# Turning activations in a transformer block: transposes inside the quadrants, and the quadrants exchanged by sixteen SBUF transfers

## The reference

```
h = rms_norm(x, g);  proj = h @ w_in;  gates = sigmoid(h @ w_gate)
merged = g_ret * (ret @ w_ret) + g_att * (att @ w_att)
x = x + merged @ w_out
u = square(relu(rms_norm(x, g2) @ w_up))       # 2048 -> 8192
x = x + u @ w_down                             # 8192 -> 2048
return rms_norm(x, g_final)
```

## Time and profile before

| what | value |
|---|---|
| median of 3 runs | 1591.18 us (1590.75 to 1592.46) |
| span of the profiled execution | 1587.2 us; no own time of it is given beside the span, the runs' median is 4.0 us above it |
| TensorE busy | 1567.3 us, 99% |
| VectorE busy | 1101.6 us, 69% |
| ScalarE busy | 739.1 us, 47% |
| DMA | 301.40 MB, mean 190 GB/s |

### The profile page before, as it was taken

The page is one execution under the profiler, slowest core; times in us unless marked ns, Lnnn a source line. Parts: engine busy times, 40 slices in busy tenths (PEclk is TensorE's granted clock), DMA queues, the critical chain, the costliest instruction groups (busy, mean ns, idle before and its releaser), DMA issues.

```text
span 1587.2 us, 18857 instructions
## 1 busy us (share of the span) xinstructions
PE 1567.3 (99%) x6992; PEld 1292.0 (81%) x6992; DVE 1101.6 (69%) x1398; ACT 739.1 (47%) x983; POOL 10.8 (1%) x17
## 2 busy tenths in 40 slices
PE   9999999999999999999999999999999999999998
PEld 7877778888888888888878888888888888888886
DVE  7877777544447776666699888458864687548855
ACT  6455555444444454444444444444444445444443
POOL 0000000000000000000000000000000000000000
PEclk9999999999999999999999999999999999999999
DMA  9645454565655555556555665565656565555562
GB/s 365 197 134 160 157 159 151 179 201 185 232 179 185 185 190 173 187 192 211 198 201 193 206 209 186 190 199 183 197 189 201 175 203 188 200 194 183 189 203 89
DMA packets 149606, 301.40 MB, mean 190 GB/s; under 512 B 4784, under 2 KB 4912, under 8 KB 149040
## 3 DMA queue, kind: packets, MB, share of 16 engines
q1 hardware_dynamic: 149120, 299.65, 57.0%
q10 hardware_dynamic: 432, 1.02, 0.2%
HBM read 298.55 MB, written 2.10 MB: 189 GB/s over the span
## 4 chain that ended last, share of the span: by engine, by line
PE 88%; DVE 8%; issue 2%; ACT 1%; DMA 0%; SPq 0%; POOLq 0%; DVEq 0%; POOL 0%; ACTq 0%
PE acc L371 85%; DVE buf L887 3%; DVE wlo L878 2%; DVE qbd L887 1%; PE sps L383 1%; PE pps L401 1%; ACT buf L591 0%; ACT whi L584 0%; DMA raw<-in_w_in 0%; PE pps L394 0%; DVE buf L1245 0%; DVE tb_lo L926 0%; DVE ta_lo L1273 0%; PE tps L427 0%; ACT prob L610 0%
## 5 line engine op out<-in xcount | busy, mean ns | idle before, releaser
L878 DVE TENSOR_TENSOR wlo<-raw,whi 128x1024 fp32r<-128x1024 f32 x544 | 662.6, 1224 | 444.9 <-ACT whi L584 442.0
L584 ACT ACTIVATE whi<-raw 128x1024 fp32r<-128x1024 f32 x544 | 573.0, 1059 | 720.5 <-PE acc L371 718.8
L371 PE MATMUL acc<-whi,ta_hi 128*128 128x512 f32 x1312 | 517.2, 394 | 2.5 <-DVE wlo L878 1.6
L371 PE MATMUL acc<-whi,ta_lo 128*128 128x512 f32 x1312 | 511.2, 390 | 0.0
L371 PE MATMUL acc<-wlo,ta_hi 128*128 128x512 f32 x1312 | 510.7, 389 | 0.0
L371 PEld LDWEIGHTS acc<-whi,ta_hi 128*128 128x128 f32 x1312 | 246.4, 188 | 55.8 <-issue 3.9
L371 PE MATMUL acc<-whi,tb_hi 128*128 128x512 f32 x736 | 287.7, 391 | 2.6 <-DVE tb_lo L926 2.6
L371 PEld LDWEIGHTS acc<-wlo,ta_hi 128*128 128x128 f32 x1312 | 246.4, 188 | 52.0 <-issue 1.7
L371 PEld LDWEIGHTS acc<-whi,ta_lo 128*128 128x128 f32 x1312 | 246.3, 188 | 51.6
L371 PE MATMUL acc<-whi,tb_lo 128*128 128x512 f32 x736 | 286.4, 389 | 0.0
L371 PE MATMUL acc<-wlo,tb_hi 128*128 128x512 f32 x736 | 286.4, 389 | 0.0
(11 more groups left out here) (128 smaller groups left out, 659.4 us busy)
## 6 DMA issues: line engine op xcount, KB each, us to landing
raw<-in_w_in SPq DMA_DIRECT2D x67, 1024.0 KB, 5.2
raw<-in_w_up SPq DMA_DIRECT2D x64, 1024.0 KB, 5.2
raw<-in_w_down SPq DMA_DIRECT2D x64, 1024.0 KB, 5.0
raw<-in_w_gate SPq DMA_DIRECT2D x32, 1024.0 KB, 5.3
raw<-in_w_att SPq DMA_DIRECT2D x16, 1024.0 KB, 5.0
raw<-in_w_ret SPq DMA_DIRECT2D x16, 1024.0 KB, 5.0
raw<-in_w_out SPq DMA_DIRECT2D x16, 1024.0 KB, 5.1
xt<-in_x_t SPq DMA_DIRECT2D x8, 256.0 KB, 8.8
```

The costliest lines, as they stand in the source:

```text
L371: last = nc.tensor.matmul(acc[B.parity][:, t, :], a[:, k, tok], b[:, slot, :], start=(k == 0 and n == 0), stop=(k == KCH - 1 and n == 2))
L584: nc.scalar.activation(whi[:, s:s + UCH, :], raw[:, u * UCH:(u + 1) * UCH, :], ACT.Copy).then_inc(hi_ready, 1)
L878: V_.tensor_tensor(wlo[:, s:s + UCH, :], raw[:, u * UCH:(u + 1) * UCH, :], whi[:, s:s + UCH, :].bitcast(f32), ALU.subtract).then_inc(lo_re ...
```

## The change

The turn is made in two steps. First VectorE transposes inside the quadrants: `squares` has four instructions of 128 partitions x 256 elements; each turns every 32 x 32 square where it lies and gathers the squares whose channels belong to quadrant o. The result goes into a fourth buffer (`place`: buf[0], in the MLP buf[2]). Then ScalarE's queue issues sixteen SBUF-to-SBUF transfers (`cross`), each of 32 partitions x 1 KB, which bring piece o of quadrant i to quadrant o, piece i of buf[1] (`crossed`). A new semaphore t_square tells that the squares are written; t_full now counts the landings (16 for each transfer). The readers go through views of the new order of buf[1] (`turned`, `tokens`), and `gain` becomes four TENSOR_SCALARs, one for each 128 channels. ScalarE's later readers of t_full that only needed the source to be free wait on t_square. `cross` stands between two of ScalarE's splits: of units 6 and 7 in stages 3 and 4, of 5 and 6 in stages 5 and 6. VectorE's split of unit 7 now comes behind the low part in stages 5 (first block) and 6, and behind the gain in stage 5. In stage 6 ScalarE makes the high part after all splits, as before.

```
+        T_DMA = (P // SQ) ** 2 * 16
+        crossed = buf[1][:].rearrange("p t n -> p (t n)").rearrange("p (i f) -> p i f", i=P // SQ)
+        turned = crossed.rearrange("p i (m r) -> p m i r", r=SQ)
+        def tokens(chunks):
+            return chunks.rearrange("p k (t i r) -> p (k t) i r", t=TILES, r=SQ)
# ScalarE
+            def cross(turn, place):
+                pieces = place[:].rearrange("p t n -> p (t n)").rearrange("p (o f) -> p o f", o=P // SQ)
+                act.wait_ge(t_square, turn + 1)
+                if later(turn):
+                    act.wait_ge(t_free, turn)
+                for i in range(P // SQ):
+                    for o in range(P // SQ):
+                        act.dma_start(crossed[SQ * o:SQ * (o + 1), i, :],
+                                      pieces[SQ * i:SQ * (i + 1), o, :]).then_inc(t_full, 16)
             def hi_from_turned(turn, dst, g):
-                act.wait_ge(t_full, turn + 1)
-                nc.scalar.activation(dst[:, ds(g * GCH, GCH), :], turned, ACT.Copy).then_inc(t_hi, 1)
+                act.wait_ge(t_full, turn * T_DMA + T_DMA)
+                nc.scalar.activation(tokens(dst[:, ds(g * GCH, GCH), :]), turned, ACT.Copy).then_inc(t_hi, 1)
# ScalarE, tail3 (stage 3); stage4 alike with B = G
-                split(B, 4, 8)
+                split(B, 4, 7)
+                cross(j + T_STAGE3, buf[0])
+                split(B, 7, 8)
# ScalarE, stage 5
-                split(B, 5, 7)
+                split(B, 5, 6)
+                cross(T_STAGE4 + 3 if j == 0 else T_STAGE5 + j - 1, buf[0])
+                split(B, 6, 8)
...
-                split(B, 7, 8)
# ScalarE, stage 6
-                        act.wait_ge(t_full, q * 4 + (T_STAGE6 + i - 1))
+                        act.wait_ge(t_square, q * 4 + (T_STAGE6 + i - 1))
                     scaled_relu(B[i - 1])
-                    split(B[i], 4, 8)
+                    split(B[i], 4, 6)
+                    cross(q * 4 + (T_STAGE6 + i - 1), buf[2])
+                    split(B[i], 6, 8)
                     hi_from_turned(q * 4 + (T_STAGE6 + i - 1), tb_hi, i - 1)
# VectorE
-            def split_and_turn(B, u0, u1, before, src, ready, n):
...
+            def squares(turn, src, place):
+                if later(turn):
+                    dve.wait_ge(t_full, turn * T_DMA)
+                view = place[:].rearrange("p t n -> p (t n)").rearrange("p (o m t r) -> p o m t r", o=P // SQ, t=TILES, r=SQ)
+                src = src.rearrange("p t (m o s) -> p o m t s", o=P // SQ, s=SQ)
+                for o in range(P // SQ):
+                    last = V_.transpose(view[:, o], src[:, o])
+                last.then_inc(t_square, 1)
             def gain(turn, dst, gains, g):
-                dve.wait_ge(t_full, turn + 1)
-                gsl = gains[:, ds(g * GCH, GCH)].unsqueeze(2).to_broadcast([P, GCH, S])
-                V_.tensor_tensor(dst[:].rearrange("p t (k n) -> p (t k) n", n=S), turned, gsl, ALU.mult).then_inc(t_free, 1)
+                dve.wait_ge(t_full, turn * T_DMA + T_DMA)
+                gsl = gains[:, ds(g * GCH, GCH)]
+                out = dst[:].rearrange("p t (k n) -> p (t k) n", n=S)
+                for m in range(GCH):
+                    last = V_.tensor_scalar(tokens(out[:, m:m + 1, :]), turned[:, TILES * m:TILES * (m + 1)],
+                                            gsl[:, m:m + 1], None, ALU.mult)
+                last.then_inc(t_free, 1)
# VectorE, stage 4; stage 3 alike (units 5 to 7 after the squares)
-                    split_and_turn(G, 4, 8, j + (T_STAGE4 - 1), buf[3][:], m_ready, j)
+                    split(G, 4, 5)
+                    dve.wait_ge(m_ready, j)
+                    squares(j + (T_STAGE4 - 1), buf[3][:], buf[0])
+                    split(G, 5, 8)
                     lo_from_turned(j + 4, tc_hi, tc_lo, j - 1)
# VectorE, stage 6 (stage 5 alike, from mix into buf[0], with the gain)
-                    split_and_turn(B[i], 4, 8, q * 4 + (T_STAGE6 + i - 1), buf[0][:], u_ready, q * 4 + i)
+                    dve.wait_ge(u_ready, q * 4 + i)
+                    squares(q * 4 + (T_STAGE6 + i - 1), buf[0][:], buf[2])
+                    split(B[i], 4, 7)
                     lo_from_turned(q * 4 + (12 + i), tb_hi, tb_lo, i - 1)
+                    split(B[i], 7, 8)
```

More of the change, by code:

```diff
@@ L216, in build @@
         turned_1 = sem("turned_1")
-        t_full, t_free = sem("t_full"), sem("t_free")
+        t_square, t_full, t_free = sem("t_square"), sem("t_full"), sem("t_free")
         ret_full, ret_read = sem("ret_full"), sem("ret_read")
@@ L252, in last_slot @@
             return ring[:, u * UCH:(u + 1) * UCH, :] if u < UNITS // 2 else spare[part][:, u * UCH - KCH // 2:(u + 1) * UCH - KCH // 2, :]
-        turned = buf[1][:].rearrange("p t (m n) -> p (t m) n", n=S)
+        crossed = buf[1][:].rearrange("p t n -> p (t n)").rearrange("p (i f) -> p i f", i=P // SQ)
+        turned = crossed.rearrange("p i (m r) -> p m i r", r=SQ)
+        def tokens(chunks):
+            return chunks.rearrange("p k (t i r) -> p (k t) i r", t=TILES, r=SQ)
         def gained(u):
@@ L772, in stage4 @@
                 else:
-                    split(G, 0, 8)
+                    split(G, 0, 7)
+                    cross(j + (T_STAGE4 - 1), buf[0])
+                    split(G, 7, 8)
                     hi_from_turned(j + (T_STAGE4 - 1), tc_hi, j - 1)
@@ L803, in _ @@
                     if j == 1:
-                        act.wait_ge(t_full, T_STAGE4 + 4)
+                        act.wait_ge(t_square, T_STAGE4 + 4)
                     residual_squares(Block(B5 + j - 1), j - 1, x1_sq)
-                split(B, 5, 7)
+                split(B, 5, 6)
+                cross(T_STAGE4 + 3 if j == 0 else T_STAGE5 + j - 1, buf[0])
+                split(B, 6, 8)
                 if j == 0:
@@ L902, in to_qbd @@
                 return qbd[o:o + SQ].rearrange("p m (t c) n -> p m t c n", t=TILES)[:, :, :, i // CHUNK, at:at + SQ]
-            def split_and_turn(B, u0, u1, before, src, ready, n):
[L906 to L911, removed]
-            def gain(turn, dst, gains, g):
-                dve.wait_ge(t_full, turn + 1)
-                gsl = gains[:, ds(g * GCH, GCH)].unsqueeze(2).to_broadcast([P, GCH, S])
-                V_.tensor_tensor(dst[:].rearrange("p t (k n) -> p (t k) n", n=S), turned, gsl, ALU.mult).then_inc(t_free, 1)
+            def squares(turn, src, place):
[6 more added lines that the diff above has]
+                last.then_inc(t_square, 1)
+            def gain(turn, dst, gains, g):
+                dve.wait_ge(t_full, turn * T_DMA + T_DMA)
[5 more added lines that the diff above has]
+                last.then_inc(t_free, 1)
             def lo_from_gained(n, src, hi, lo, g, done):
@@ L925, in lo_from_turned @@
                 dve.wait_ge(t_hi, n)
-                V_.tensor_tensor(lo[:, ds(g * GCH, GCH), :], turned, hi[:, ds(g * GCH, GCH), :].bitcast(f32),
+                V_.tensor_tensor(tokens(lo[:, ds(g * GCH, GCH), :]), turned, tokens(hi[:, ds(g * GCH, GCH), :].bitcast(f32)),
                                  ALU.subtract).then_inc(t_free, 1)
@@ L1134, in tail3 @@
                 dve.wait_ge(gated_ready, j + 1)
-                for u in range(5, 8):
-                    turn(by_chunk(buf[3][:]), to_tokens(turned), 4 * (u - 5), 4 * (u - 4))
-                    split(B, u, u + 1)
+                squares(j + T_STAGE3, buf[3][:], buf[0])
+                split(B, 5, 8)
             def after3(j, B):
-                turn(by_chunk(buf[3][:]), to_tokens(turned), 12, 16, t_full)
                 split(B, 0, 1)
@@ L1179, in merge @@
                 mine.wait(dve)
-                dve.wait_ge(t_full, j + T_STAGE4)
                 V_.tensor_tensor(buf[3][:], buf[2][:], acc[0][:], ALU.mult).then_inc(evacuated[0], 1)
@@ L1225, in _ @@
                 if j == 0:
-                    split_and_turn(B, 4, 6, T_STAGE4 + 3, buf[3][:], m_ready, 4)
-                    split(B, 6, 7)
+                    dve.wait_ge(m_ready, 4)
+                    squares(T_STAGE4 + 3, buf[3][:], buf[0])
+                    split(B, 4, 7)
                     lo_from_turned(8, tc_hi, tc_lo, 3)
@@ L1230, in _ @@
                     prev = Block(B5 + j - 1)
-                    split_and_turn(B, 4, 6, T_STAGE5 + j - 1, mix[:, :, (j - 1) * COLS:j * COLS],
-                                   evacuated[prev.parity], prev.turn + 1)
+                    dve.wait_ge(evacuated[prev.parity], prev.turn + 1)
+                    squares(T_STAGE5 + j - 1, mix[:, :, (j - 1) * COLS:j * COLS], buf[0])
+                    split(B, 4, 7)
                     gain(T_STAGE5 + j - 1, buf[2], gffn, j - 1)
-                    split(B, 6, 7)
+                if j:
+                    split(B, 7, 8)
                     lo_from_gained(8 + j, buf[2], ta_hi, ta_lo, j - 1, h2T_ready)
-                split(B, 7, 8)
+                else:
+                    split(B, 7, 8)
                 if j == GROUPS:
```

## The result

The changed kernel takes 1697.14 us (median of 4, 1693.38 to 1698.41) against 1590.97 us (median of 4 of before): ratio 1.0665, 95% interval 1.0651 to 1.0679, 106 us more. My forecast was 1604.6 us with a range up to 1640: the right sign, the right queue, and a size eight times too small (13.4 against 106 us).

The account below looks back on a forecast made before the run. TensorE's matmul pace was taken as the bound. Late splits and turns from ScalarE's held queue cost MLP 9.2, w_out 3.9 and merge 0.3, sum 13.4 us: span 1600.6, plus 4.0 to the runs' median, 1604.6 us; range 1589 to 1640.

Parts of the forecast that it names:

- What bounds the kernel, and the worth of the removed work: TensorE's matmul pace bounds the span; VectorE loses 146 us of work, worth only up to 5.1 us.
- the 5.1 us of stalls: TensorE's old waits for a turn's low part in MLP and w_out, all that a faster turn could give back.
- The path: ScalarE's in-order queue holds back late splits and the turn: MLP 9.2, w_out 3.9, merge 0.3, retention 0 us.
- my line for a pitch of 0.50: At 0.50 us between issues, all 28 turns stall at unit 6 or 7: +36 us, 1627 us.
- A landing: Time for a crossing's piece to land: 2.2 us taken, bounds 1.2 and 5.2.
- The price of an issue: Each of sixteen transfers per turn holds ScalarE's queue 0.45 us, 7.2 us a crossing; bounds 0.37 and 0.60.
- The rival with a pitch of 0.60: Queue throttles: slowly landing pieces pace ScalarE's issues, making units 6 and 7 late: +83 us, 1674 us; chance 0.12.
- The slope: How time moves with issue pitch: 0.42 gives about +5 us, 0.50 gives +36 us; threshold close, hence the wide range.
- The clock: TensorE's pace of 0.2271 us a matmul was taken as unchanged; no term for it in the sum.
- A small step the other way: MLP crossing start on ScalarE, placed at T + 6.7 after unit 5's split; T is the block's first matmul.

Follow-up runs that it names:

- the best version: Changed kernel with quadrants exchanged through HBM by five SyncE transfers, w_out's first-block store issued ahead of queued loads; against the kernel before: 1585.91 us, ratio 0.9981.

## Why the prediction was wrong

- **What bounds the kernel, and the worth of the removed work.** Right. The transposes over 128 partitions took 412 ns (436 forecast), VectorE lost 161 us (146 forecast), and in the best version that was worth what the 5.1 us of stalls allow: it came out 3.4 us under the kernel before. The gain took 4 x 0.347 = 1.39 us (1.3 forecast).
- **The path.** Right: ScalarE's queue, the late splits, the low part of the turn. At my price the MLP's twelve other turns would have missed only unit 7, and retention and three turns of w_out nothing; TensorE waited in all 28, at unit 7 in retention and merge and at unit 6 elsewhere, as my line for a pitch of 0.50 has it. A landing was 1.8 us at the least and 2.4 in the median (2.2 forecast).
- **The price of an issue.** This is the failed step: "I take 0.45 us: 16 x 0.45 = 7.2 us for a crossing", with bounds 0.37 and 0.60. It was 0.64 us and 10.14 us, over the upper bound. The rows had only issues with HBM on one side, and except at the start only single ones. SBUF on both sides adds some 0.15 us, and standing in a row some 0.1. The rival with a pitch of 0.60 gave 1674 us and had 0.12; its mechanism (the queue throttles) was wrong, since the price is the same on an empty chip, and its working is near what happened (its terms add up to 82 and not 83, and by the same working unit 7 in merge and retention comes 2.35 us late and not 3). The estimate of 0.43 us that I had set beside it from the Trainium skill (DMA: Bandwidth & Descriptors, the table under "Why a DMA increments its semaphore by 16 and not by 1", with the clock from Advanced Engine Details and Errata, "Clock Domains") is as far off here as mine; it agrees with what an issue from HBM took in a row (0.442).
- **The slope.** "With 0.50 ... +36 us" was right in kind: eight, twelve and sixteen pieces (2, 17 and 106 us) show how steep it gets. I saw it, and the range still ended at 1640, far short of what my own upper bound of 0.60 gives.
- **The clock.** Missing from the working: "if TensorE's pace of 0.2271 us changes, which nothing here suggests". I priced a stall by its length; on top of 72 us of stalls come 29 us in the matmuls behind them, at least 21 of them at half the clock. With this term my own line for a pitch of 0.60 (82 us) ends at 111, near the 106 measured.
- **A small step the other way.** The crossing began at T + 5.77 and not T + 6.7: the first issue goes out 0.13 us after ScalarE's split of unit 5 has started (1221.75 and 1221.88), it doesn't wait for the end of it. This took 0.9 us off every late split, so a part of the missing price was given back by another error.

## What to carry to other kernels

Count the issues of an added transfer on the queue that issues them, each at the price of its kind (0.64 us in a row with SBUF on both sides, 0.47 with HBM on one), and lay the sum against the lead of the work behind it; below the lead it cost next to nothing here (2 us with eight pieces), above it every turn pays. Where many small pieces go, one large transfer through HBM and a few back can be cheaper than a direct exchange; here it did best on the queue of the large loads, ahead of them. When TensorE will stall for microseconds, add what its clock takes afterwards.

## What the runs showed of the hardware

- A transfer's issue costs by its kind: 0.514 us alone and 0.612 in a row for SBUF to SBUF, 0.32 to 0.40 alone and 0.44 to 0.45 in a row from HBM, nearly the same from ScalarE and SyncE (612 and 591 ns), for 32 or 128 partitions, for 6 KB, 32 KB or 128 KB. From GpSimd it was 498 ns, but its transfers landed 4.1 us (median) to 5.2 us later, against 1.8 to 1.9 from ScalarE.
- ScalarE's first issue goes out while the element operation ahead of it still runs (0.13 us after its start at 1221.75).
- A stall of TensorE has an aftermath. After 4.05 us of it the granted clock was 0.57 over 3.6 us, and the same pace of 0.427 us followed each of the six longest stalls of this trace (3.9 to 6.6 us). After stalls of about 2 us it differed: the clock stayed at 1.00 after the one of 2.09 us that ended at 1373.15, and was 0.57 after the one of 2.03 us that ended at 546.12. What decides between the two is open.

```profile
1373.00:1376.60 3.60, 3.43 (x14) 2.55 (x15) 2.93 (x4) 3.03 (x4) 0.00 (x0) 1.00 0.00 0
546.00:549.60 3.60, 3.48 (x9) 2.79 (x10) 3.36 (x7) 2.10 (x3) 0.00 (x0) 0.57 0.66 193
```
